# Scan stage of an RWKV-7 layer: products joined over 128 partitions, and a moved first own-values product

## The reference, cut to what matters

```python
def rwkv_step(S, inp):
    r, w, k, v, a, b = inp
    sa = jnp.einsum('bdhvk,bdhk->bdhv', S, a)
    S = S * w[..., None, :] + sa[..., None] * b[..., None, :] + v[..., None] * k[..., None, :]
    return S, jnp.einsum('bdhvk,bdhk->bdhv', S, r)

def rwkv_scan(S0, prep):
    xs = (both_directions(prep['r'], False), both_directions(prep['decay'], True),
          both_directions(prep['k_dir'], True), both_directions(prep['v'], False),
          -both_directions(prep['kk'], False),
          both_directions(prep['kk'][:, :, None] * prep['iclr'], True))
    S, ys = lax.scan(rwkv_step, S0, xs)
```

## Time and profile before

| | |
|---|---|
| median of 3 runs | 2538.04 us |
| profiled execution | 2535.24 us |
| its span (first to last instruction) | 2533.4 us |
| scan stage, first to last PE work of its pairs | about 671 to 1029 us of the span |
| mean granted TensorE clock | 0.920 |

### The profile page before, as it was taken

How to read it: one execution, slowest core, us unless ns; L and a number is a source line. 1 busy time by engine, 2 the same in 40 slices (tenths; PEclk the granted TensorE clock), 3 DMA queues, 4 the chain that set the end, 5 groups by cost and what they waited for, 6 DMA issues and landing times.

```text
span 2533.4 us, 40846 instructions
## 1 busy us (share of the span) xinstructions
PE 2013.9 (79%) x16281; PEld 1230.6 (49%) x16281; DVE 1661.4 (66%) x3506; ACT 853.6 (34%) x1682; POOL 680.0 (27%) x577
## 2 busy tenths in 40 slices
PE   5999947888678788887899887777777777778877
PEld 3766635666667776575455432333333333333332
DVE  4699964687034344554776777777777777777764
ACT  4666633465434343223223222222222121212121
POOL 0000020000112121002344445444444444444441
PEclk8999978988689999898999999999989999988999
DMA  6477653523443231436999999999999999999995
GB/s 240 155 254 250 224 204 143 186 72 117 176 166 140 104 137 45 169 117 242 421 420 415 383 420 416 420 421 419 421 419 421 420 421 419 421 420 421 421 421 214
DMA packets 136029, 742.01 MB, mean 293 GB/s; under 512 B 17920, under 2 KB 25120, under 8 KB 69280
## 3 DMA queue, kind: packets, MB, share of 16 engines
q0 software_dynamic: 73728, 536.90, 51.1%
q1 hardware_dynamic: 60960, 200.41, 21.8%
q10 hardware_dynamic: 1152, 2.10, 0.2%
HBM read 683.67 MB, written 55.69 MB: 292 GB/s over the span
## 4 chain that ended last, share of the span: by engine, by line
DMA 30%; PE 15%; DVE 4%; issue 3%; ACT 2%; POOL 0%; DVEq 0%; ACTq 0%
DMA uv<-in_uv_in,ic 30%; PE bank L2654 13%; DVE junk L2539 2%; DMA scores_dram<-later 1%; PE bank L92 1%; PE bank L94 1%; PE bank L93 1%; ACT dg L2451 1%; PE bank L2635 1%; POOL uv L2374 0%; DVE wql L2503 0%; ACT ge L2446 0%; ACT L2446 0%; DVE gc_ L2544 0%; ACT L2291 0%
## 5 line engine op out<-in xcount | busy, mean ns | idle before, releaser
L2654 PE MATMUL bank<-uv,dg 128*128 128x512 f32 x1664 | 816.1, 648 | 212.2 <-ACT dg L2451 212.1
L2654 PEld LDWEIGHTS bank<-uv,dg 128*128 128x128 f32 x1664 | 335.4, 206 | 682.8 <-issue 404.3
L2374 POOL DMA_INDIRECT uv<-in_uv_in,ic x416 | 478.2, 1150 | 627.8 <-PE bank L2654 556.5
L2539 DVE SCALAR_TENSOR_TENSOR junk<-uv,gr 128x1024 f32<-128x1024 f32 x416 | 510.1, 1226 | 185.7 <-DMA uv<-in_uv_in,ic 158.1
L2446 ACT ACTIVATE ge<-dt_ 128x4 f32<-128x4 f32 (+1 forms) x130 | 26.7, 205 | 945.1 <-DVE junk L2539 945.0
L2654 PE MATMUL bank<-uvx,dg 128*128 128x512 f32 x384 | 185.7, 641 | 52.5 <-ACT dg L2451 52.5
L2451 ACT ACTIVATE dg<-ident,gc_ 128x128 f32<-128x128 f32 x512 | 163.9, 390 | 31.2 <-DVE gc_ L2544 29.1
L2539 DVE SCALAR_TENSOR_TENSOR junk<-uvx,gr 128x1024 f32<-128x1024 f32 x96 | 117.7, 1226 | 58.6 <-DMA uvx<-in_uv_in,ic 56.0
L2654 PEld LDWEIGHTS bank<-uvx,dg 128*128 128x128 f32 x384 | 76.4, 204 | 161.7 <-issue 90.1
L2374 POOL DMA_INDIRECT uvx<-in_uv_in,ic x96 | 114.5, 1193 | 120.8 <-PE bank L2654 110.4
L92 PE MATMUL bank<-hx_hi,wzh 128*128 128x512 f32 x160 | 70.5, 440 | 34.9 <-DVE wzl L984 19.4
(11 more groups left out here) (362 smaller groups left out, 3704.7 us busy)
## 6 DMA issues: line engine op xcount, KB each, us to landing
pair_record<-rec SPq DMA_DIRECT2D x32, 768.0 KB, 4.9
wt<-in_wrow_in SPq DMA_DIRECT2D x32, 512.0 KB, 4.4
wraw<-in_wpair_in SPq DMA_DIRECT2D x24, 512.0 KB, 3.6
xb<-pair_record SPq DMA_DIRECT2D x16, 768.0 KB, 6.2
wm<-in_wmod SPq DMA_DIRECT2D x4, 2048.0 KB, 20.9
wz<-in_wz_in SPq DMA_DIRECT2D x32, 256.0 KB, 3.3
wraw<-in_wq_in SPq DMA_DIRECT2D x16, 512.0 KB, 6.4
uv<-in_uv_in,ic POOLq DMA_INDIRECT x416, 28.1
```

What stands on the lines that cost most here:

```text
L2374: pool.indirect_dma_start(ring(i), None, g["uv_in"], bass.IndirectOffsetOnAxis(ap=ic[:, s % ICR, k:k + 1], axis=0)).then_inc(su[row_slot[i ...
L2539: dve.scalar_tensor_tensor(junk[:, :], ring(i)[:, 0:D], 1.0, hc[:, t % 2, :], ALU.mult, ALU.mult, accum_out=dt[:, k:k + 1]).then_inc(s_ud, 1)
L2654: mm = pe.matmul(acc(t, c)[:, :], dg[:, n % 2, k, :], ring(i)[:, D + 512 * c:D + 512 * c + 512], start=h == 0 and q == 0 and k == 0, stop= ...
```

## The change

Four edits that go together.

1. **Layout.** The record keeps k and b of a chunk pair interleaved as k0, b0, b1, k1 (`kb`), stored and loaded as one field; `invert` loads b out of it in pieces of 128 elements. v, a and the two r buffers become one tile `var`, so that a and r of a chunk can be streamed together. Decayed k and b are written over v and a, four POOL instructions of half size.
2. **Joined products.** `products(j, 0)` is k by a for the context alone; `products(j, 1..4)` have [k, b] (128 columns) against [a, r] (128 streamed columns), and one of the four results is not used. `updates` and `outputs` contract [k; b] with [v; pw] over 128 partitions in one call, where two accumulated calls of 64 stood; `carried` makes a transition and its gg part at once; the context's `transitions` stand alone.
3. **Copies.** So that the halves land on the right partitions, ACT copies v transposes in two halves, k/b transposes in two pieces and each `weighted` in three; DVE masks in 34 small instructions (before 12).
4. **Order.** `own(j+1, 0)` and `own(j+1, 1)` stand at step 7, the last six turns at steps 8 to 10. `turned` waits for bank 4's readers.

```diff
@@ project
-                        stored("k", j - 1)
...
-                        stored("b", j - 1)
+                        sp.wait_ge(s_k, 2 * j)
                         sp.wait_ge(s_b, 2 * j)
+                        stored("kb", j - 1)
@@ invert
-                    for i, o in enumerate((RC_A, RC_B)):
...
+                    sp.dma_start(ab[:, j % 2, 1, :, :, :].rearrange("p d (c w) s -> p (d c) (w s)", w=2), record[j, :, RC_K:RC_V].rearrange(
+                        "p (e w s) -> p e (w s)", w=4, s=CHUNK)[:, :, CHUNK:3 * CHUNK]).then_inc(s_ab[j % 2], 16)
@@ scan, GpSimd
+                    for d in range(NDIR):
+                        if d:
+                            pool.wait_ge(s_t, 12 * j + 6)
+                            pool.wait_ge(s_a, 2 * NR * j + 2 * NR)
...
+                        for w in (slice(0, 4, 3), slice(1, 3)):
+                            pool.tensor_tensor(dkb[:, d, :, w, :], kb[:, d, :, w, :], wide, ALU.mult).then_inc((s_kp, s_bp)[d], 1)
@@ scan, ScalarE
+                    for p in range(2):
+                        act.activation(vp[HALF[1 - p], 2 * r:2 * r + 2, p, :, :], src[HALF[1 - p], :, :, 0, :], ACT.Copy).then_inc(s_pwc, 1)
+                    act.activation(pa[:, 2 * r:2 * r + 2, :, :], src[:, :, :, 1, :], ACT.Copy).then_inc(s_pwc, 1)
@@ scan, VectorE
+                        for p in range(2):
+                            dve.tensor_tensor(ka[HALF[p], e:e + 2, h, :], src[HALF[p], :, p, 0, :],
+                                              mgt[HALF[p], :].unsqueeze(1).broadcast_to((64, 2, CHUNK)), ALU.mult).then_inc(s_am, 1)
+                        for d in range(NDIR):
+                            b = src[:, d, :, 1, :]
+                            dve.tensor_tensor(kr[:, e + d, :, h, 1, :], b[:, :, ::-1] if d else b,
+                                              (mge, mgr)[d][:, :].unsqueeze(1).broadcast_to((P, 2, CHUNK)), ALU.mult).then_inc(s_am, 1)
@@ scan, TensorE
+                    pe.wait_ge(s_am, NA * j + 8 * n - 6)
...
+                                mm = pe.matmul(bank[h][:, o:o + P], kb[HALF[h], d, cp, 2 * p:2 * p + 2, :].rearrange("p q s -> p (q s)"),
+                                               var[HALF[h], 1:3 + j % 2:1 + j % 2, d, 2 * cp + p, :], start=True, stop=True)
...
-                        for lhs, rhs, q in ((kt, vt[:, e, :, :], 0), (bt, pw[:, e, :, 0, :], 1)):
+                        for p in range(2):
                             for h in range(2):
...
+                                mm = pe.matmul(bank[p][HALF[h], HEAD * x:HEAD * x + HEAD], kr[:, e, p, h, 0, :], vp[:, e, p, h, :],
+                                               start=True, stop=True)
...
+                                mm = pe.matmul(bank[MG[r][p]][HALF[h], P * x:P * x + P], pa[HALF[1 - p], e, h, :],
+                                               kr[HALF[1 - p], e, p, h, :, :].rearrange("p q k -> p (q k)"), start=True, stop=True)
...
-                            if c < 5:
+                            if c <= NR:
                                 products(j + 1, c - 1)
...
+                            if c < 7:
                                 turn(j + 1, c - 1)
-                            elif c < 9:
-                                turn(j + 1, 2 * c - 6)
-                                turn(j + 1, 2 * c - 5)
-                    if j < NPAIR - 1:
-                        own(j + 1, 0)
-                        own(j + 1, 1)
+                            elif c == 7:
+                                own(j + 1, 0)
+                                own(j + 1, 1)
+                            else:
+                                turn(j + 1, 2 * c - 10)
+                                turn(j + 1, 2 * c - 9)
```

More of the change, by code:

```diff
@@ new lines, in middle @@
+                    for r in range(2):
+                        c0 = CC + 4 * r
+                        for p in range(2):
+                            dve.wait_ge(s_m, 6 * j + 2 * r + p + 3)
+                            src = bank[MG[r][p]][:, :].rearrange("p (c d w) -> p c d w", c=2, d=2)
+                            o = mt[:, c0 + p:c0 + 4:2, :, :]
+                            dve.tensor_tensor(o, src[:, :, :, 0:HEAD], o, ALU.add).then_inc(s_mc, 1)
+                            for d in range(NDIR):
+                                own = lr[j % 2][:, d, 4 * r + p:4 * r + 4:2, :]
+                                dve.tensor_tensor(gg[:, p, 2 * r:2 * r + 2, d, :], src[:, :, d, HEAD:], own[:, :, ::-1] if d else own,
+                                                  ALU.add).then_inc(s_gc, 1)
@@ L1784, in products @@
                         if j:
-                            pe.wait_ge(s_gc, 4 * j)
-                    else:
-                        pe.wait_ge(s_am, 12 * j + (2, 6, 8)[n - 1])
+                            pe.wait_ge(s_nc, 4 * j)
+                        for x in range(NE - NL):
+                            cp, d = divmod(x, 2)
+                            for p in range(2):
+                                for h in range(2):
+                                    mm = pe.matmul(bank[h][HALF[p], CHUNK * x:CHUNK * x + CHUNK], kb[HALF[h], d, cp, 3 * p, :],
+                                                   la[HALF[h], d, 2 * cp + p, :], start=True, stop=True)
+                                    if x == NE - NL - 1 and p == 1:
+                                        mm.then_inc(s_a, 1)
@@ L1892, in updates, with carried @@
+                                if x == CC - 1 and h == 1:
                                     mm.then_inc(s_m, 1)
-                def carried(j):
-                    pe.wait_ge(s_nc, 4 * j + 4)
-                    for x in range(NL):
+                def carried(j, r):
+                    if r:
+                        pe.wait_ge(s_mc, 6 * j + 3)
+                        pe.wait_ge(s_gc, 8 * j + 2)
+                    else:
+                        pe.wait_ge(s_pwc, 18 * j + 18)
+                    for x in range(4):
+                        e = NE - NL + 4 * r + x
@@ L1969, in _ @@
                     turn(0, n)
-                for n in range(1, 4):
+                for n in range(1, NR):
                     products(0, n)
-                for n in range(3, 12):
+                for n in range(3, 6):
                     turn(0, n)
@@ L1975, in _ @@
                 own(0, 1)
+                for n in range(6, 12):
+                    turn(0, n)
                 for j in range(NPAIR):
@@ L1982, in _ @@
                     updates(j, 0)
+                    transitions(j)
+                    carried(j, 0)
                     updates(j, 1)
-                    carried(j)
+                    carried(j, 1)
                     outputs(j)
```

281 lines of the change are left out of this document (126 added, 155 removed).

## The result

The changed kernel takes 2548.91 us (median of 13 runs, 2541.38 to 2556.57) where the kernel before takes 2537.2 (13 runs, 2525.53 to 2546.11) on the same chip: a ratio of 1.0044, interval 1.0030 to 1.0057. It is slower by 0.4%, where I forecast 1.1% faster, and it lies outside my range. The profiled execution took 2551.01 with a span of 2549.2, which is 15.8 more than before's 2533.4.

A forecast was written before the change was run, and what follows sets the result against it. Dense stretches were taken as bound by instruction count, step stretches by the chain PE, DVE, PE. Dense -39.4, last -4.2, first -7, steps +18.2, elsewhere +4.7 total -27.7: 2507.5 us, 2510 on the medians' scale; range 2490 to 2540.

The forecast's parts named there:

- What bounds the dense stretch: Dense stretch of scan: bound by instruction count, a block of 256 costing PE at least 3.7 us.
- Rival (2): Dense stretch: issue stops don't follow the instruction count, 5.8 us a pair instead of 0.7; +41, 2551 us; chance 0.05.
- The unknown tile: Updates and outputs, 80 calls over 128 partitions: no row shows this tile; taken at 0.12 us for two calls, 4.8 us.
- rival (1): Updates and outputs: column halves run one after the other, 0.24 us a pair of calls; +38, 2548 us; chance 0.11.
- What is left of the stops: Dense stretch: block stops that remain after the change, 0.7 us, within a stretch of 16.5 us.
- The step stretch: Step stretch: products and masks alternate in rounds of 2.9 us, 21.5 against 18.88, so +2.6 a pair, +18.2 in all.
- The price of a mask: Step stretch, DVE: eight masks a round at 0.20 us each, from a 128-element add's start-to-start; 0.28 the upper bound.
- One dip now costs nothing there: Step stretches before: 18.84 us at clock 0.91, 19.19 at 1.00, so a lower clock costs nothing.
- Rival (3): Step stretches: smaller gain, masks at 0.28 each (+18) or lower clock more often; 2528 to 2531 us; chance 0.12.
- Moving `own` frees nothing by itself: Step stretch: own's 1.75 us stand at step 7 instead of the end, and later turns fill the rest.
- The first pair: First pair of scan: -7 us in its dense stretch with the longest stop, +1.3 for four rounds with nothing between.
- Elsewhere: Outside the stretches: project's larger last store +1.9, invert's load in pieces +1.5, first pair's rounds +1.3; +4.7 us.

The follow-up runs named there:

- e3: Kernel before with each two 64-column calls in updates and outputs made one of 128, 80 calls fewer a pair, timing only; 2498.5 us, ratio 0.9838.
- e13: Kernel after with eight masks a round kept, all on 128 partitions, some writing an unread tile, timing only; 2523.5 us, ratio 0.9951 to before.
- e1: Kernel after with the ka masks of both partition halves in one instruction, six masks a round instead of eight, timing only; 2510.29 us, ratio 0.9891 to before.
- e2: Kernel after with the o_lo subtraction (lowered) moved from step 5 to after state add 8; 2537.14 us, ratio 0.9991 to before.
- e5: Kernel before with the new order alone: own at step 7, last six turns at steps 8 to 10; 2527.26 us, ratio 0.9942.
- e11: e10 with own put back after step 10 and the turns in the order of the kernel before; 2505.58 us, ratio 0.9869 to before.
- e10: Kernel after with step-stretch products all on separate 64 x 64 tiles; joined updates, carried, outputs and new order kept; 2495.75 us, ratio 0.9832 to before.

## Why the prediction was wrong, point by point

**What bounds the dense stretch: right.** A stretch of 224 calls instead of 340 is 4.65 us shorter; halved calls alone (e3) give 4.06. Rival (2), that the stops don't follow the count, falls: they are 35.8 us over before's seven stretches, 13.2 over e3's. The work was also right: PE is busy for 15.5 to 16.0 us at the full clock, against 15.5 in the sum.

**The unknown tile: right.** PE's timeline, a dense stretch:

```profile
881.64 1.15 PE L1898 MATMUL bank<-vt_pw,kbt_rkb 128*64 128x64 f32 x32
```

32 matmuls are 16 calls, or eight pairs, in 1.15 us, of which some 0.22 is the last one's own: 0.12 a pair, where rival (1) had 0.24. Two column halves of full height go side by side.

**What is left of the stops: mis-sized.** I had 0.7 us a pair. They are 11.9 us between 743.11 and 978.55, 2.0 for each of the six pairs: none in the first stretch, where PE waits 1.48 us for ScalarE's copy of `nn` instead, and one or two of up to 2.3 us in each of the others.

```profile
885.99 0.33 PE L1922 MATMUL bank<-kbt_rkb,pw_a 64*64 64x128 f32 x2 [2.11 <-issue]
```

One more stretch, 870.67 in the windows, has a clock of 0.91 and 1.7 us more of PE's time. Together the dense stretches gave 32.6 where the sum has 43.6. The last one, with no loads beside it, has no stop and takes 15.81. Its six sisters have a DMA share of 0.62 to 0.70, where before's had 0.35; that the denser loads make the instruction packets late would fit the last stretch, but not the first, which has the highest share (0.70) and no stop. It wasn't tried, and the cause of what remains stays open. The Trainium skill ("Runtime: NRT & Kernel Launch", section Instruction fetch mechanics) calls block crossings mostly hidden. With 3.5 blocks in 15.8 us they are, in the last stretch; with 5.4 blocks in before's 20.2 they weren't: some 3 us of it are stops.

**The step stretch: the term that failed.** I had +2.6 and it is +6.0 a pair, 41.9 in all instead of 18.2. Its parts:
- The price of a mask. "Eight masks of 128 elements, priced by the start-to-start of a 128-element add, 0.20": that row has 128 partitions, four of the eight masks have 64, and they cost 0.32. Four rounds of 0.5 are 2.0 a pair. The mean of the eight is 0.26, within my bounds of 0.20 and 0.28, and I had taken the lower end for all of them. e13 shows that the form is what counts: as many instructions with more elements in them take the 0.20. Whether it is the 64 partitions or the change from one half to the other, it leaves open.
- `lowered`, "adds 0.6". It added 1.5, as the later masks put it behind a GpSimd pair that it had not met before. That is 0.9 a pair, shown by e1, e2 and e13, which all have it at 0.68.
- The clock. "One dip now costs nothing there" was said of before's stretches, in which PE had slack. In after's PE is on the chain with each round, and three stretches with a granted clock of 0.93, 0.87 and 0.87 take 25.73, 26.90 and 26.89 instead of 24.18: 7.0 us. PE's busy time is longer by nearly as much (20.08 against 17.48). There isn't more of the lower clock than before (from 700 us to the end of the last step stretch PE was granted 1.2 GHz for 23.9 us in both), it only falls where it costs. No experiment tried it. e1 and e13 have a dip in their first step stretch alone (0.91 and 0.93), and e2 has one of 0.96, at the beginning of a stretch that takes the usual 22.71, so not every dip there costs.
- The first of the seven, with no `lowered` of a pair before it, is 21.96. That is 2.2 less and sets off a part of the others.

What was right in it is the structure: the rounds alternate, PE waits at each for the last mask, and with the masks at the assumed price the stretch is the forecast one (21.36 in e13, 21.5 in the text). Rival (3) had the dearer masks, and with 18 us even more than the 14 that they cost. It had nothing of `lowered`, and of the clock it had "more often", which didn't come.

**"Moving `own` frees nothing by itself": wrong.** It frees 0.9 us of each step stretch (e5, e11). The two waits in before's stretch, 0.58 and 0.40, stood in its timeline, and I counted work there instead of waits. So the change without its order would have done worse.

**The first pair: -7 and +1.3, measured +1.4.** The long stops did go: 1.43, 4.92 and 2.42 us before, 2.03 and 0.67 after. But its four rounds have no other work between them, and at a granted clock of 0.82, 0.61, 0.50 and 0.64:

```profile
684.18 1.38 PE L1824 MATMUL bank<-lvar,lkb 64*128 64x128 f32 x16 [2.25 <-DVE kbt_rkb L1721]
```

From the first `r` products to `own` are 16.4 us (680.06 to 696.46), where before had 12.8 (676.70 to 689.48), and PE's first product, which waits for the loads, comes 1.3 later into the stage (8.2 us instead of 7.0). The joined load of k and b, 1.5 MB, stands ahead of that of a in the queue, where 768 KB stood; I had no term for that in the first pair. The remaining 2.6 are not accounted for.

**Elsewhere, +3.4 without the first pair: measured +5.1.** `project` 1.9 for 1.9 forecast; `invert` +0.3 for 1.5, though its first load was waited for 10.88 instead of 10.18 us; what follows `scan`, at which I had nothing, +2.5, which is no more than stages differ by from one profile to another (the first stage alone ends between 48.6 and 54.9 us in these kernels).

**The sum.** Missed were 23.7 in the step stretches, 11.0 in the dense ones, 7.1 in the first pair and 1.7 elsewhere: 43.5, from -27.7 to +15.8. My range ended at 2540, since I let the misses come one at a time, each from the forecast: the masks at their upper bound gave 2528. All four groups missed to the same side, and the largest of the misses hangs on a price that I had put at the lower end of its bounds.

## What to carry to other kernels

Count the instructions of a dense TensorE stretch before its columns, and join calls there; where a chain through VectorE sets the pace, count VectorE's instructions instead, and leave the products in the form that lets the masks be few, wide and over all 128 partitions. Here the change was worth -1.7% with the joined form kept only where it pays (e10), and +0.4% with it in both places, both with the new order; without the order the former was -1.3% (e11). Price an instruction by a row of its own form, with the same number and start of partitions and the same instruction ahead of it, and for each instruction that a longer chain delays, look up which other engine is at work at its new time.

## What the runs showed of the hardware that I had not expected

- A VectorE mask of 128 elements on 64 partitions cost more than one on 128 partitions: 0.32 us from start to start against 0.20. The mask on 128 partitions at 850.89 lasts 0.29, and the next starts at 851.10, before its end. The two on 64 partitions start at 850.25 and 850.56, and each time the next instruction starts only 0.03 after their end. But the one at 851.29, behind a mask on 128 partitions, starts 0.20 after it. So what is dear is to stand behind a mask on 64 partitions, or to begin at another partition than the instruction ahead: both hold at the same places, and no run here separates them.
- A VectorE subtract of two SBUF tensors took 1.54 us instead of 0.68 when it began 0.48 us behind a GpSimd multiply, and 0.68 when it began 0.01 us ahead of one.
- A 64 x 128 tile with 64 streamed columns takes as long as one with 128. 16 calls take 2.00 us, eight of 128 columns 1.16; less some 0.27 for the last one's own time, that is 0.11 a call for both. The same products as 32 calls on 64 x 64 tiles take 1.16, 0.03 a call.
- 80 one-column calls a pair in the dense stretch cost as much as the 64-column calls that they stand for (23.59 us a stretch against 22.66), more of it in PE's busy time and less in issue stops.
